# Experts' sums made with channels in the partitions: the weighted rows stationary, the put matrix moving

## The reference

```python
def hier_moe(x, wg, bg, we, be, w1, w3, w2):       # top-1 group, top-2 experts in it
    ...
    h = jax.nn.silu(xb @ w1[e]) * (xb @ w3[e])     # per block of rows of expert e
    return h @ w2[e]
    ...
    out = jnp.zeros_like(xt).at[row_tok].add(ys * row_w[:, None])
...
f = hier_moe(x, ...)
x = layer_norm(DEEPNORM_ALPHA * x + f, ln2_g[i], ln2_b[i])
```

## Time and profile before

| what | us |
|---|---|
| median of 3 runs (2852.53 to 2860.73) | 2858.66 |
| the profiled execution | 2852.64 |
| its span in the trace | 2850.8 |
| PE busy | 2612.3 (92%) |
| DVE, ACT, POOL busy | 1031.4, 831.5, 901.9 |
| adding in the loops, L1067, busy | 250.4, 1008 records |
| idle time before L1082, ended by a DMA | 11.7 |

### The profile page before, as it was taken

One profiled execution on the slowest core, in us unless ns is written; L12 is line 12 of the kernel. 1 busy time (PEld: TensorE's weight loads), 2 busy tenths in 40 slices (PEclk: granted clock), 3 DMA queues, 4 the chain that ended last, 5 costly groups with the idle time before them and its releaser, 6 DMA issues.

```text
span 2850.8 us, 44871 instructions
## 1 busy us (share of the span) xinstructions
PE 2612.3 (92%) x18042; PEld 1979.0 (69%) x18042; DVE 1031.4 (36%) x2418; ACT 831.5 (29%) x1428; POOL 901.9 (32%) x373
## 2 busy tenths in 40 slices
PE   8999999999999999999989799998978679999996
PEld 7996566999999766699989544444457574444443
DVE  3411534543441153454235532323224533232323
ACT  4430312444443131244333211111114522212112
POOL 6870002688787100268867000000016230000000
PEclk9999999999999999999999899999988989999998
DMA  7543412455554331245454799999943058999994
GB/s 237 165 156 119 133 60 89 130 173 163 179 174 159 110 114 60 75 132 178 152 148 134 301 420 421 421 421 421 419 164 100 30 211 359 421 421 421 421 421 200
DMA packets 271213, 643.95 MB, mean 226 GB/s; under 512 B 16865, under 2 KB 191073, under 8 KB 221665
## 3 DMA queue, kind: packets, MB, share of 16 engines
q1 hardware_dynamic: 268000, 635.66, 59.5%
q10 hardware_dynamic: 2176, 3.15, 0.4%
q0 software_dynamic: 896, 3.15, 0.4%
HBM read 637.72 MB, written 4.19 MB: 225 GB/s over the span
## 4 chain that ended last, share of the span: by engine, by line
PE 77%; DMA 11%; DVE 7%; ACT 2%; issue 1%; SPq 0%; ACTq 0%; POOL 0%; DVEq 0%
PE bank L551 36%; DMA wring<-in_exp_w 11%; PE bank L515 10%; PE bank L1082 6%; PE bank L1067 5%; PE bank L644 5%; PE bank L1093 3%; PE bank L1043 3%; PE bank L1056 3%; PE bank L736 1%; PE bank L584 1%; PE bank L809 1%; DVE XN_rounded L1530 1%; DVE ARENA L1924 1%; PE bank L525 1%
## 5 line engine op out<-in xcount | busy, mean ns | idle before, releaser
L1976 POOL TENSOR_TENSOR wring_rounded<-wring,wring_rounded 128x1024 fp32r<-128x1024 f32 (+1 forms) x336 | 873.5, 2612 | 342.7 <-ACT wring_rounded L1159 342.2
L551 PE MATMUL bank<-SQ_rounded,wring_rounded 128*128 128x272 f32 (+1 forms) x3456 | 655.0, 289 | 28.4 <-POOL wring_rounded L1976 17.7
L551 PEld LDWEIGHTS bank<-SQ_rounded,wring_rounded 128*128 128x128 f32 x3456 | 546.3, 190 | 30.7 <-POOL wring_rounded L1976 13.7
L551 PE MATMUL bank<-XN_rounded,wring_rounded 128*128 128x272 f32 (+1 forms) x1728 | 498.2, 288 | 0.0
L1159 ACT ACTIVATE wring_rounded<-wring 128x1024 fp32r<-128x1024 f32 (+1 forms) x336 | 374.8, 1116 | 374.4 <-PE bank L551 369.3
L551 PE MATMUL bank<-ARENA_rounded,wring_rounded 128*128 128x272 f32 (+1 forms) x3456 | 445.4, 291 | 20.9 <-DVE ARENA_rounded L1694 8.6
L551 PEld LDWEIGHTS bank<-ARENA_rounded,wring_rounded 128*128 128x128 f32 x3456 | 440.1, 191 | 24.7 <-DVE ARENA_rounded L1694 9.0
L551 PEld LDWEIGHTS bank<-XN_rounded,wring_rounded 128*128 128x128 f32 x1728 | 329.4, 191 | 0.2
L1082 PE MATMUL bank<-wring,ARENA 128*32 128x512 f32 x2048 | 246.2, 598 | 42.0 <-DVE ARENA L1924 30.3
L1428 ACT ACTIVATE ARENA<-bank 128x512 f32<-128x512 f32 x128 | 76.5, 597 | 672.2 <-PE bank L1082 672.2
L1067 PE MATMUL bank<-ARENA 64*128 64x512 f32 x1008 | 250.4, 615 | 0.0
(11 more groups left out here) (243 smaller groups left out, 2481.4 us busy)
## 6 DMA issues: line engine op xcount, KB each, us to landing
wring<-in_exp_w SPq DMA_DIRECT2D x256, 1024.0 KB, 18.6
ARENA<-in_exp_w SPq DMA_DIRECT2D x128, 1024.0 KB, 17.1
wring<-in_ffn_w_gate SPq DMA_DIRECT2D x44, 1024.0 KB, 5.5
wring<-in_ffn_w_up SPq DMA_DIRECT2D x44, 1024.0 KB, 8.1
wring<-in_ffn_w_down SPq DMA_DIRECT2D x32, 1408.0 KB, 6.2
wring<-in_w_in SPq DMA_DIRECT2D x16, 2048.0 KB, 7.8
wring<-in_conv_w_in SPq DMA_DIRECT2D x24, 512.0 KB, 5.4
wring<-in_attn_w_in SPq DMA_DIRECT2D x5, 2048.0 KB, 9.1
```

The source lines that it names most:

```text
L551: ins = nc.tensor.matmul(o, rounded(a_[:, k, cols]), rounded(x), start=(start and k == 0 and j == 0), stop=(stop and k == len(tiles) - 1 a ...
L1976: st.done(nc.gpsimd.tensor_tensor(rounded(low), low, part(high), ALU.subtract), wl_ready)
```

## The change

The roles in the adding are exchanged. `YS`'s 64 rows by 128 channels are stationary, and `PUT`'s 64 rows by 256 tokens are moving, eight matmuls per expert instead of four (`put_tile`). The sums stand with channels in the partitions: bank k//2 holds channel tiles k and k+1 for k even, 256 tokens each. The eight go in the order `PUT_ORDER`, which takes the two halves of the rows by turns. After the loop, the copies to `YT`, the 16 transposes and `sum_from` are gone; DVE adds the residual straight from banks 0 to 3, in the order `SUM_ORDER`, and releases a bank after two tiles. The mean over channels takes the tiles in the same order, and the layer norm after the experts uses banks 4 and 5 instead of 0 and 1. `YT` no longer takes up space.

```diff
+PUT_ORDER = (0, 4, 1, 5, 2, 6, 3, 7)
+SUM_ORDER = (0, 1, 4, 5, 2, 3, 6, 7)
...
-            def layer_norm(b):
+            def layer_norm(b, order=range(KD)):
...
-                for k in range(KD):
+                for i, k in enumerate(order):
                     st.need(sum_tile)
-                    ins = nc.tensor.matmul(bank[b][:, 0:SEQ], const("mean_d"), R2[:, k, :], start=(k == 0),
-                                           stop=(k == KD - 1))
+                    ins = nc.tensor.matmul(bank[b][:, 0:SEQ], const("mean_d"), R2[:, k, :], start=(i == 0),
+                                           stop=(i == KD - 1))
...
-                def put(b, u, first, last):
+                def put_tile(k, u, first=False, last=False):
+
+                    r0, at = 64 * (k // 4), k % 2 * SEQ
+                    return nc.tensor.matmul(bank[k // 2][:, at:at + SEQ], YS[r0:r0 + 64, k % 4 * P:k % 4 * P + P],
+                                            PUT[r0:r0 + 64, u % 2, :], start=first and k % 2 == 0,
+                                            stop=last, skip_group_check=True)
+
+                def put(b, u, first):
 
                     pe.wait_ge(m.ys, b + 1)
                     pe.wait_ge(m.put, b + 1)
-                    for t in range(2):
-                        for dh in range(2):
-                            ins = nc.tensor.matmul(bank[2 * t + dh][:, :], PUT[64 * dh:64 * dh + 64, u % 2, t * P:(t + 1) * P],
-                                                   YS[64 * dh:64 * dh + 64, :], start=first, stop=last,
-                                                   skip_group_check=True)
+                    for k in PUT_ORDER:
+                        ins = put_tile(k, u, first)
                     ins.then_inc(m.added, 1)
...
-                for b in range(4):
-                    t, dh = b // 2, b % 2
-                    ins = nc.tensor.matmul(bank[b][:, :], PUT[64 * dh:64 * dh + 64, (GROUP - 1) % 2, t * P:(t + 1) * P],
-                                           YS[64 * dh:64 * dh + 64, :], start=False, stop=True, skip_group_check=True)
-                    st.done(ins, bank_full["act"][b])
-                    held[b] = "act"
-                for b in range(4):
-                    claim(b)
-                for k in range(KD):
-                    turns(4 + k % 4, "dve", "dve",
-                          [(bank[4 + k % 4][:, t * P:(t + 1) * P], YT[:, t, k * P:(k + 1) * P]) for t in range(2)])
+                for k in PUT_ORDER:
+                    ins = put_tile(k, GROUP - 1, last=True)
+                    if k % 2 == 1:
+                        st.done(ins, bank_full["dve"][k // 2])
+                        held[k // 2] = "dve"
...
-                for b in range(4):
-                    copy(YT[:, b // 2, b % 2 * 512:b % 2 * 512 + 512], b, bank[b][:, :])
...
-                for k in range(KD):
-                    sum_from(4 + k % 4, k)
+                for i, k in enumerate(SUM_ORDER):
+                    b, at = k // 2, k % 2 * SEQ
+                    if i % 2 == 0:
+                        st.need(bank_full["dve"][b])
+                    st.done(STT(R2[:, k, :], X2[:, k, :], ALPHA, bank[b][:, at:at + SEQ], ALU.mult, ALU.add), sum_tile)
+                    if i % 2 == 1:
+                        mark(bank_free["dve"][b])
...
-            layer_norm(0)
+            layer_norm(4, SUM_ORDER)
```

More of the change, by code:

```diff
@@ L475, in build_model @@
         DG, ROWS, GS, PC, SLC, CMB = a(8, P), a(4, SEQ), a(2, P), a(GROUP), a(4), a(MORE)
-        YT, SCR8 = a(2, D), a(2, 8)
+        SCR8 = a(2, 8)
         W2B = a(GROUP, 2048)
@@ L1096, in group @@
                         if not (peeled and u == 0):
-                            put(b - 1, (u - 1) % GROUP, peeled and u == 1, False)
+                            put(b - 1, (u - 1) % GROUP, peeled and u == 1)
                 group(0)
@@ L1452, in _ @@
             experts(0)
-            layer_norm(0)
+            layer_norm(4)
             attention()
@@ L1958, in _ @@
             experts(0)
-            layer_norm(0, "ln2g", "ln2b", 0)
+            layer_norm(4, "ln2g", "ln2b", 0)
             x_at["attention"] = st.sent[x_tile]
@@ L1963, in _ @@
             experts(1)
-            layer_norm(0, "ln2g", "ln2b", 1)
+            layer_norm(4, "ln2g", "ln2b", 1)
             x_at["end"] = st.sent[x_tile]
```

## The result

The changed kernel takes 2839.91 us (median of 6 runs, 2838.11 to 2844.69), the kernel before 2858.22 us beside it (6 runs, 2852.53 to 2864.53). The ratio is 0.9945, 95% interval 0.993 to 0.996: 18.3 us faster, where 8.3 were forecast. The direction was right, the size less than half of what came.

The account below looks back on a forecast made before the run. Experts' stages bound by weight DMAs (29.8 us a group against PE's 28.7), with uncovered parts behind each loop. Loops 0, exits 0, tails -4.3 and -4.0 sum to -8.3 us: 2850 predicted, range 2841 to 2864.

Parts of the forecast that it names:

- The adding in the loop, term 0: Experts' loops: eight steps of 0.216 us take 0.01 us more an expert, inside PE's spare time, so 0.
- the loads show: Rival, adding in the loop: weight loads not hidden, 0.11 us more in seven steps; 2864 partly, 2941 in full; chance 0.08.
- PE's spare time, 6.2 and 5.8 us: Experts' stages, layers 0 and 1: PE's wait for weights; longer experts cost nothing up to there, and count 64-fold beyond.
- The tails, -4.3 and -4.0: Last adding's start to DVE's subtraction, layers 0 and 1: without copies and transposes, 4.3 and 4.0 us less.
- The sums were hidden: Behind layer 0's loop: DVE's sums start half-way through the adding and are hidden with 1.2 us to spare.
- The exits, term 0: Last adding of the loop to down product: stalls of 5.47 and 5.35 us stay; bounds 5.4 either way each.
- The clock, term 0 with up to 3 us either way: Layer 0's end and attention: TensorE's clock changes at other points of the work, up to 3 us either way, taken as 0.
- down to add: Down product to last adding, behind each layer's loop: forecast 0.
- more than the sum: Rival, attention or exits: clock periods there fall favourably, -12 to -14 us, 2845; chance 0.08.
- the sum: Whole kernel: 0 in the loops, 0 for the exits, -4.3 and -4.0 behind them, together -8.3 us.

Follow-up runs that it names:

- The runs with 0.43 and 0.96 us more an expert: Changed kernel with two of each expert's eight adding matmuls made twice, 2895.36 us; changed kernel with four matmuls of one row half, then four of the other, 2942.72 us.
- after: The changed kernel itself, with the new adding and the two loops, against the kernel before: 2839.91 us, ratio 0.9945.
- the two single-loop kernels: One loop over the groups in place of two, each group under a condition: in the changed kernel 2838.32 us, in the kernel before 2842.11 us.
- 160 instructions: Kernel before the change with 160 increments of an unused semaphore on PE ahead of layer 0's first gather: 2865.16 us, ratio 1.0028.
- another whose PE instructions are the same in number: Changed kernel with SUM_ORDER = (6, 7, 2, 3, 4, 5, 0, 1), so that DVE waits for the bank filled last: 2837.55 us, one run.

## Why the prediction was half right

*The adding in the loop, term 0: right.* It was to take 1.93 us to the next up product and did; the rival "the loads show" wanted 0.11 more for each of seven steps. The rule of the Trainium skill ("TensorE: Matmul & The Clock Gate", part 3), that a load overlaps with matmuls in flight only when its row group differs, is not borne out: in each step both halves of the rows are streaming and both are loaded, and the step still lasts 0.216 us. The run that gives the two halves in blocks shows that order matters (+0.96 us), but there too 2.89 us is less than 16 records in a row.

*PE's spare time, 6.2 and 5.8 us: right*, to about 1 us. The runs with 0.43 and 0.96 us more an expert lengthened the stages of after by 21.5 and 22.4, and by 55.4 and 55.0 us, which is 64 times the excess less 5 to 6.5.

*The tails, -4.3 and -4.0: right at equal clock.* Layer 0 gave -4.41, both at half clock behind the exit. At full clock throughout, the two single-loop kernels give 9.98 and 10.01 against 5.69, -4.3 in each layer. The sums were hidden, 0.7 us of it by the order of the banks.

*The exits, term 0: wrong, and this is the step that failed.* I argued: "The two stalls read alike though they lie at different places of the program, so I take no change". Two places are too few. The stalls read alike because both happened to land badly; the program with 16 more matmuls in each body landed better, which nobody had aimed at: it was luck. Measured: -5.67 us in the two layers. The reason that I took from "Runtime: NRT & Kernel Launch", instruction fetch mechanics, of the Trainium skill, that a branch whose target isn't loaded waits for a fetch, is borne out: each such exit has a packet of instructions at its start, and PE goes on 1.8 to 2.7 us after the start of the packet that it needs. My reading of it, that a longer body can only keep or lengthen the stall, was wrong: with 16 matmuls more it halved, and with 8 more than that it was back.

*The clock, term 0 with up to 3 us either way: it gave about 2 us, inside that bound, and it hung on the exit.* In layer 1 the clock stayed up in this profile, so that its tail was 5.69 and its down to add 1.86. Of the 5.99 of its tail, 1.7 are the clock's, and 0.87 ahead of it. The excess of the traces over the forecast, 16.1 - 8.3 = 7.8 us, is thus: exits 5.7, tail of layer 1 2.0, down to add 0.3, tail of layer 0 0.1, less 0.3 of loops and attention. The median's 18.3 agrees with 16.1 within its interval (11 to 20).

*The rival that happened* is "more than the sum", exits and clock falling favourably, at 2845 and a chance of 0.08. It had the right mechanism, too little weight, and too small a size: it went 3.7 to 5.7 us beyond the sum, which has room for one stall of 5.4 or for the clock, and the traces went 7.8 beyond it, with exits and clock together.

So what is the change worth? With the code's place out of it (one loop in both), 2842.11 to 2838.32, 3.8 us by the medians. The traces give 2 x 4.3, less 0.6 for exits that are 0.3 longer each: 8.0. The runs spread over 5.5 us before and 9.5 after, and the two estimates aren't reconciled. By neither are more than 8.0 of the 18.3 us the new adding's and tail's own; the rest came from how PE's program happened to lie against its packets, and from the clock which that kept up.

Open: where the packets' borders lie in the program, which no trace tells, and with it why layer 1's exit stayed long where 160 instructions mended layer 0's. Open too is why layer 1's exit is 2.48 in one program and 5.87 in another whose PE instructions are the same in number. The traces show how the two differ, and not why: both have 105 packets of instructions in all, but between layer 1's first gather and the exit the kernel after took four of them and the other three, and the one that was lacking came behind the exit, ahead of the down product. So how far PE has read ahead when the loop starts to turn counts beside the length of the program.

## What to carry to other kernels

A change that adds or removes instructions moves all code behind it: before crediting a gain of a few tenths of a per cent to the change, compare the "issue" rows at loop exits and jumps in both traces, look for packets of instructions beside them, and try the same layout on the old kernel. A rarely used second loop is better folded into the first, with its body under a condition, than jumped over: here that was 15.6 us for an edit of three lines, where the loop had time to spare for the condition. A pause of TensorE costs more than its length, because the matmuls behind it may run at half clock. The fastest version with more than one run has both edits, 2838.3 us, though its lead over the changed kernel (2839.9) is within the runs' spread.

## What the runs showed of the hardware that was not expected

- From the last adding's start to the down product, with a jump past a loop that never ran between them, it took PE 4.3 to 4.8 us or 7.3 to 8.1, and nothing between (20 exits); with 64 more instructions ahead, both exits went from the one to the other. Past a body that has just run, with four empty rounds, it was 3.2 to 3.5.
- Behind exits of 5.2 us and more the granted clock was 0.50 every time, for 6.8 to 13.7 us; behind 2.4 to 2.9 in six of eight; behind 1.3 to 1.7 (six exits, four of them of kernels with one loop) never.
- PE went on 1.8 to 2.7 us after the start of the 16 KB packet of instructions that it waited for, and where it waited for two, the second started 3.1 to 3.7 us after the first (20 exits).
- A semaphore increment as an instruction of its own takes PE 0.15 us (55 in 8.4 us).
- Eight pairs of records that share the rows by turns take 1.93 us, in two blocks 2.89.
